# The MLP's residual in a two-block transformer kernel: turned by VectorE in 32 by 32 blocks and moved by transfers, in place of 32 transposes by TensorE

## The chip, the cores and the metric

The kernel runs on one core of a Trainium2 chip. The metric is the device time of one execution in microseconds; the median of three runs of the kernel before is 989.25 us (988.41 to 989.67). The profiled execution took 988.87 us, its span (first to last recorded instruction) 987.0 us, at a mean granted TensorE clock of 0.997 of full speed.

## The reference

The reference is two blocks on a sequence of 512 rows of 1024 features, float32. The first is a windowed attention with a gated spatial branch. The second puts a mixer ahead of an MLP. The change touches the last step of the second block alone:

```
h = h + y @ w_out[l]                        # x1 in this text
u = _rmsnorm(h, mlp_norm_g[l])
h = h + jnp.square(jax.nn.relu(u @ w_up[l])) @ w_down[l]
h = _rmsnorm(h, final_norm_g)
```

`w_up` is 1024 x 4096, `w_down` 4096 x 1024. The residual is the first `h` of the third line: x1, 512 rows by 1024 features. (The second block has 16 further rows at its front for the mixer; the MLP works on 512.)

## The kernel before

**Float32 products in parts.** Each operand is split into a high part (fp32r) and a low part, the difference to it, and a product is three matmuls: high by high, high by low, low by high. ScalarE casts the high part of each weight tile (`cast`), VectorE or GpSimd subtracts for the low part (`w_low`, `low`).

**The layout.** Up to the MLP, activations lie with features on partitions: x1 is `F3`, 128 features by 512 rows in each of eight slices `F3[:, n]`. The down product turns the layout: its result has rows on partitions, and so has the output. The residual must therefore be transposed before it can be added to the down product. It is put into `Y` (the memory `F1f`), which holds 128 rows by 4 x 1024 values: half of the rows r, half of the features c, tile of rows t, 512 features n.

**The MLP's order.** The hidden features are worked in four parts of 1024. In each part there are eight up tiles (`up_tile(part, n)`, 24 matmuls each), then seven down products (`down_tile(part, n, h)`, named P11, P_7, P12, P_5, P_6, P_3, P_4; 24 matmuls each), seven in place of eight since the 2 x 2 grid of halves is multiplied in Strassen's way. Sums and differences of operands for it are made by VectorE (`x_sums`, `w_sum`) and by accumulating loads that GpSimd issues (`w_sum` in `gpsimd_program`). VectorE drains each up tile from PSUM (`act`), ScalarE squares it (`act_square`), casts the operand's high part (`a_high`), VectorE makes the low part (`a_low`). Down products P11, P_7, P_5 and P_6 are gathered in `acc`, which lies in the memory `F4f`; P12 adds to `Y`. Their output copies are `out(part, n)` on VectorE.

**The residual before.** TensorE transposes x1 after the up tiles 3, 4, 5 and 6 of part 0, two slices of four 128 x 128 transposes each time (`residual` in `tensor_program`, line 941), into PSUM banks 6 and 7; ScalarE copies each into `Y` (`residual` in `scalar_program`, line 1481; in the profile its copies stand under the helper's line 1021 as Fm<-ps).

**What sets the order.** The order on each engine is written out by hand, and each engine does its list in order; semaphores by name tie them (`w.wait_ge(name, key)`). The first two down weights' high parts (tile `m` 0 and 1) go into `w_more`, which is the memory of `F3`; so their cast waits until x1 has been read for the last time (before: `residual_turned` 7). The first output copy, `out(0, P11)`, writes `acc[0]`. The down product P12 may begin when the output copies of P11 have emptied its banks (`down_free`). ScalarE's list for the stage is in the loop `for n in range(3, 8)`: a cast for up tile n + 2, the two residual copies, squares, and in rounds 5 and 6 `a_high` for P11 and P_7; then the casts of the down weights with squares 5 and 6 between.

**Other transfers in the stage.** SP loads weight blocks of 1 MB when the low parts that read the slot's old content are made (line 433), and quarters of w_down (lines 512, 520). GpSimd issues an accumulating load of 512 KB each between its low parts (line 2564). Earlier in the kernel, at line 508, SP loads the input x once more in pieces of 32 floats, four transfers of 32 x 128 such pieces, and VectorE turns them 32 by 32 (line 1976, `x_again`).

Of the kernel before, what the change touches and what calls it, by code (L numbers as in the profile page):

```python
# [117 lines left out]
J_IN2, J_CG, J_OUT2, J_UP = 82, 92, 96, 104  # L118
# [13 lines left out]
def build(nc, t):  # L132
    with ExitStack() as ctx:
# [150 lines left out]
        Z = X[:].rearrange("p k n -> p (k n)").rearrange("p (t c) -> p t c", t=4)  # L284

        Y = F1f.rearrange("p (r c t n) -> p r c t n", r=2, c=2, t=2)
        Hl_flat = Hl[:].rearrange("p k n -> p (k n)")
        by4 = lambda ap: ap.rearrange("p (k n) -> p k n", k=4)
        by2 = lambda ap: ap.rearrange("p (k n) -> p k n", k=2)
# [276 lines left out]
        def tensor_program(e, w):  # L566
# [363 lines left out]
                    mm = e.matmul(ps[:, 6, :], ones_r, x, start=(n == 0), stop=(n == 1))  # L930
                mm.then_inc(*b.done("mlp_row_sums", 0))

            def residual(n):
                bk = 7 - n % 2
                if n > 1:
                    w.wait_ge("residual_set", n - 2)
                elif n == 1:
                    w.wait_ge("mlp_mean", 0)
                w.wait_ge("x1_late", n)
                for i in range(4):  # L940
                    mm = e.transpose(ps[:, bk, 128 * i:128 * i + 128], F3[:, n, 128 * i:128 * i + 128], ident[:])  # L941
                mm.then_inc(*b.done("residual_turned", n))

            def down(part, n):

                xh, xl = x_slot(part, n)
# [25 lines left out]
            def down_free(part, n, r):  # L972

                if n == P_4:
                    return "residual_set", 7 - r
                if n == P_3:
                    return "drained", up_tile(0, r)
                if n in (P11, P_7):
                    return "drained", up_tile(part, (4 if n == P11 else 6) + r)
                last = {P12: P11, P_5: P_7, P_6: P12}[n]  # L980
                return ("kept", (last, r)) if part == 3 else ("down_out", (part, last, r))

            for part in range(4):
                for n in range(8):
                    if part == 0:
                        free = (("conv_low", n) if n < 2 else ("x1_late", n) if n < 4 else ("x1_late", n - 4) if n < 6
                                else ("drained", up_tile(0, n - 4)))
                    else:
                        free = (("down_out", (part - 1, P_5 if n < 2 else P_6, n % 2)) if n < 4 else
                                ("drained", up_tile(part, n - 4)))  # L990
                    product(up_tile(part, n), [[(up_bank(part, n), 0, 512)]], A8h, A8l, lambda k: ("u3_low", k), MLP_ORDER,
                            free=[free], tail=0 if part or n else 2)
                    if part == 0 and n == 2:
                        mlp_sums()
                    if part == 0 and 3 <= n < 7:
                        residual(2 * n - 6)
                        residual(2 * n - 5)
                for n in range(7 if part < 3 else 6):
                    down(part, n)

# [18 lines left out]
        def scalar_program(e, w):  # L1019
            def copy(out, src, scale=1.0):  # L1020
                return e.activation(out, src, ACT.Copy, scale=scale)  # L1021

            def cast(j):
                blk, i = tiles[j]
                if blk is not None:
                    w.wait_ge(f"raw_in{blk % 2}", blk)
                else:
                    part, n, h = i
                    if n in (P11, P12, P_3):
                        w.wait_ge(f"quarter{int(n != P11)}{int(n == P_3)}_in", part)  # L1030
                    else:
                        by_dve = n == P_4 or (n, h) == (P_6, 1)
                        w.wait_ge(*(("w_sum_v", (part, n, h)) if by_dve else (w_sum_name(n, h), (part, n))))
                m = turn_of(j)
                before = j - 3 if m < 2 else j - 5 if m == j - J_UP - 8 else j - 7
                if in_w_last(j):
                    w.wait_ge("lo", J_UP + 22 * 3 + 7)
                elif m in (0, 1):
                    w.wait_ge("residual_turned", 7)
                elif before >= 0:  # L1040
                    group = 1 if tiles[before][0] is None else {8: 0, 4: 1, 2: 3}[tile_rows(before)]
                    w.wait_ge("products", (before, group))
                copy(w_hi(j), raw_tile(j)).then_inc(*b.done("hi", j))
# [434 lines left out]
                    w.wait_ge("mlp_sum", n - 2)  # L1478
                e.activation(sq[n % 2] if n else sq[2], F3[:, m], ACT.Square).then_inc(*b.done("mlp_square", n))

            def residual(n):
                w.wait_ge("x1_late", 3)
                w.wait_ge("residual_turned", n)
                src = ps[:, 7 - n % 2, :].rearrange("p (r t c) -> p r t c", r=2, t=2)
                copy(Y[:, :, n // 4, :, 128 * (n % 4):128 * (n % 4) + 128], src).then_inc(*b.done("residual_set", n))

            def a_high(part, n):

                if n in (P11, P12, P_4):
# [27 lines left out]
            def keep(n):  # L1517

                for r in range(2):
# [4 lines left out]
                        copy(less[n][:, r], bank, -1.0).then_inc(*b.done("less", (n, r)))  # L1524
                    copy(kept[n][:, r], bank).then_inc(*b.done("kept", (n, r)))

            for n in range(3, 8):
                if n < 6:
                    cast(up_tile(0, n) + 2)
                if n < 7:  # L1530
                    residual(2 * n - 6)
                    residual(2 * n - 5)
                for i in {3: (0,), 4: (1, 2), 5: (3,), 6: (4,)}.get(n, ()):
                    act_square(0, i)
                if n in (5, 6):
                    a_high(0, n - 5)
            cast(down_tile(0, P11, 0))
            act_square(0, 5)
            cast(down_tile(0, P11, 1))
# [75 lines left out]
        def vector_program(e, w):  # L1615
# [689 lines left out]
            def act(part, n):  # L2305
                j = up_tile(part, n)
                if n == 0:
# [3 lines left out]
                e.scalar_tensor_tensor(X[:, n], ps[:, up_bank(part, n), :], 0.0, RB, ALU.max, ALU.mult).then_inc(  # L2311
                    *b.done("drained", j))

            def x_sums(part, n):

                one, other, old = {P_7: (x_half(1, 0), x_half(0, 0), None), P_5: (x_half(1, 0), x_half(1, 1), None),
                                   P_6: (x_half(0, 0), x_sum, P_5), P_3: (x_half(0, 1), x_sum, P_6)}[n]
                w.wait_ge("act_set", (part, 3 if n == P_7 else 7))
                if old is not None:
                    w.wait_ge("a_low", (part, old))  # L2320
                elif part:
                    w.wait_ge("a_low", (part - 1, P_3))
                e.tensor_tensor(x_operand(n), one, other, ALU.subtract).then_inc(*b.done("x_sum", (part, n)))
# [22 lines left out]
            def out(part, n):  # L2346

                for r in range(2):
# [2 lines left out]
                    w.wait_ge("products", (down_tile(part, n, 1), r))  # L2351
                    signal = b.done("down_out", (part, n, r))
                    if n != P12 and part == 0:
                        e.tensor_copy(y, bank).then_inc(*signal)
                    else:
                        w.wait_ge(*(("down_out", (part - 1, n, r)) if part else ("residual_set", 7)))
                        e.tensor_tensor(y, bank, y, ALU.add).then_inc(*signal)

            def last_sum():
# [14 lines left out]
            for part in range(4):  # L2374
                for n in range(8):
                    act(part, n)
                    if part == 3 and n < 6:
# [3 lines left out]
                        if n == 5:  # L2381
                            b.value["vector_step", "spread"] = b.count["vector_step"]
                    if n == 3:
                        x_sums(part, P_7)
                    if n == 4:
                        a_low(part, P11)
# [335 lines left out]
```

## Time and profile before

| | before |
|---|---|
| median of the runs | 989.25 us |
| profiled execution, its own time | 988.87 us |
| its span | 987.0 us |
| VectorE busy | 627.5 us |
| ScalarE busy | 470.6 us |
| GpSimd busy | 524.9 us |
| residual transposes of TensorE | 32, from 669.8 to 689.7 us |
| DMA, whole span | 117.49 MB, mean 119 GB/s |

Times in rows are microseconds from the span's start unless marked ns. PE is TensorE, DVE VectorE, ACT ScalarE, POOL GpSimd; SPq and ACTq are the issuing side of SyncE and ScalarE. A duration of a single matmul is longer than the distance to the next, since they overlap. DMA issues aren't counted as busy time of their engine. A DMA share of 1 means that the packets' times add up to all 16 DMA engines; since packets overlap it can pass 1.

### The profile page before, as it was taken

What the parts mean: (1) busy time and instruction counts of PE and PEld (TensorE: products, weight loads), DVE (VectorE), ACT (ScalarE), POOL (GpSimd) and SP (SyncE); (2) the same over time, 40 slices, a digit from 0 to 9 for tenths busy, and PEclk for the clock granted to TensorE, in tenths of its full rate; (3) what the DMA queues carried; (4) which work ended last, traced back from release to release, by engine and by line L of the source; (5) the groups of instructions that cost most, each with busy time, mean ns of one, the idle gap of its engine ahead of it and who ended that gap; (6) DMA issues with size and microseconds to landing.
All of it is one profiled execution on the core that took longest, in us unless ns stands there. A gap on an engine that the chain in (4) does not pass through costs nothing.

```text
span 987.0 us, 12665 instructions
## 1 busy us (share of the span) xinstructions
PE 976.6 (99%) x4827; PEld 827.5 (84%) x4827; DVE 627.5 (64%) x938; ACT 470.6 (48%) x746; POOL 524.9 (53%) x625
## 2 busy tenths in 40 slices
PE   9999999999999999999999999999999999999996
PEld 7888888888888888888899988888888888888885
DVE  5782257665373763274669999874962771595696
ACT  4554445554673223442334866554643443353464
POOL 4555555556555895555656778555056037018212
PEclk9999999999999999999999999999999999999998
DMA  7323221212353225623223123468558347536346
GB/s 238 102 78 126 85 87 44 85 41 68 107 175 124 86 86 134 146 87 127 65 86 107 46 74 118 125 237 193 149 175 197 107 147 185 149 87 182 53 85 171
DMA packets 109116, 117.49 MB, mean 119 GB/s; under 512 B 20434, under 2 KB 86512, under 8 KB 109056
## 3 DMA queue, kind: packets, MB, share of 16 engines
q1 hardware_dynamic: 102304, 102.20, 33.1%
q0 software_dynamic: 6448, 14.16, 8.4%
q8 instruction: 38, 0.62, 0.2%
q10 hardware_dynamic: 304, 0.33, 0.1%
q14 instruction: 22, 0.18, 0.1%
HBM read 110.91 MB, written 2.10 MB: 114 GB/s over the span
## 4 chain that ended last, share of the span: by engine, by line
PE 99%; DVE 0%; ACT 0%; DVEq 0%; issue 0%; ACTq 0%
PE ps L585 70%; PE ps L967 15%; PE ps L604 4%; PE ps L730 1%; PE ps L654 1%; PE ps L751 1%; PE ps L715 1%; PE ps L714 1%; PE ps L845 1%; PE ps L1013 1%; PE ps L792 1%; PE ps L637 0%; PE ps L630 0%; PE ps L941 0%; PE ps L879 0%; DVE X L2472 0%
## 5 line engine op out<-in xcount | busy, mean ns | idle before, releaser
L2523 POOL TENSOR_TENSOR wlo<-raw,whi 128x256 fp32r<-128x256 f32 x496 | 400.4, 860 | 216.6 <-ACT whi L1021 216.5
L585 PE MATMUL ps<-Hh,whi 128*128 128x512 f32 x512 | 201.6, 394 | 0.0
L585 PE MATMUL ps<-Hl,whi 128*128 128x512 f32 x512 | 199.5, 390 | 0.0
L1021 ACT ACTIVATE whi<-raw 128x1024 fp32r<-128x1024 f32 (+1 forms) x126 | 132.2, 1050 | 87.4 <-PE ps L585 51.4
L585 PE MATMUL ps<-Ah,whi 128*128 128x512 f32 (+1 forms) x496 | 164.3, 357 | 0.0
L585 PE MATMUL ps<-Al,whi 128*128 128x512 f32 (+1 forms) x496 | 163.5, 356 | 0.0
L585 PE MATMUL ps<-Hh,wlo 128*128 128x512 f32 x512 | 129.4, 389 | 0.0
L585 PEld LDWEIGHTS ps<-Hh,wlo 128*128 128x128 f32 x512 | 96.1, 188 | 20.0
L585 PEld LDWEIGHTS ps<-Hh,whi 128*128 128x128 f32 x512 | 96.2, 188 | 19.6 <-DVE Hl L1620 0.2
L585 PEld LDWEIGHTS ps<-Hl,whi 128*128 128x128 f32 x512 | 96.2, 188 | 19.2
L585 PE MATMUL ps<-Ah,wlo 128*128 128x512 f32 (+1 forms) x496 | 104.8, 356 | 0.0
L585 PEld LDWEIGHTS ps<-Ah,whi 128*128 128x128 f32 x496 | 88.0, 188 | 13.1
L585 PEld LDWEIGHTS ps<-Al,whi 128*128 128x128 f32 x496 | 87.9, 188 | 13.0
L585 PEld LDWEIGHTS ps<-Ah,wlo 128*128 128x128 f32 x496 | 83.3, 188 | 13.3
L2564 POOL DMA_DIRECT2D w_w<-in_w_down x16 | 19.5, 1216 | 118.3 <-DVE wlo L1620 50.9
L2311 DVE SCALAR_TENSOR_TENSOR X<-ps,Rb 128x512 f32<-128x512 f32 x32 | 21.8, 688 | 86.2 <-PE ps L585 85.3
L1623 DVE TENSOR_TENSOR tmp<-ps,Rb 128x512 f32<-128x512 f32 x25 | 17.2, 690 | 59.4 <-PE ps L585 59.4
L2534 POOL TENSOR_TENSOR P<-P,sm 128x1024 f32<-128x1024 f32 (+1 forms) x16 | 26.9, 1682 | 51.9 <-DVE sm L1813 51.9
L967 PE MATMUL ps<-whi,Hl 128*128 128x512 f32 x216 | 53.3, 389 | 0.0
L585 PE MATMUL ps<-Ah,w_more 128*128 128x512 f32 x160 | 50.2, 389 | 0.0
L967 PEld LDWEIGHTS ps<-whi,Hl 128*128 128x128 f32 x216 | 40.5, 188 | 8.4
L2523 POOL TENSOR_TENSOR w_more<-raw,w_more 128x256 fp32r<-128x256 f32 x40 | 30.9, 933 | 19.5 <-ACT w_more L1021 19.5
(371 smaller groups left out, 1662.8 us busy)
## 6 DMA issues: line engine op xcount, KB each, us to landing
raw<-in_w_in SPq DMA_DIRECT2D x29, 1024.0 KB, 5.3
raw<-in_w_up SPq DMA_DIRECT2D x16, 1024.0 KB, 5.6
Fm<-in_w_down SPq DMA_DIRECT2D x8, 1024.0 KB, 5.0
w_w<-in_w_down POOLq DMA_DIRECT2D x16, 512.0 KB, 5.7
raw<-in_w_in SPq DMA_DIRECT2D x14, 512.0 KB, 3.8
raw<-in_w_att_out SPq DMA_DIRECT2D x4, 1024.0 KB, 5.2
raw<-in_w_sg_out SPq DMA_DIRECT2D x4, 1024.0 KB, 5.2
raw<-in_w_o SPq DMA_DIRECT2D x4, 1024.0 KB, 5.1
```

The source lines that it names most:

```text
L585: mm = e.matmul(ps[:, bk, 0:c1 - c0], of(j)[:, k % kk, 128 * g:128 * g + 128], x[:, k, c0:c1], start=(start and n == 0), stop=(stop and n ...
L604: mm = e.matmul(ps[:, banks[r], :], x[:, k, 128 * r:128 * r + 128], of(j)[:, k % 2], start=(i == 0 and n == 0), stop=(i == 3 and n == 5))
L654: mm = e.matmul(ps[:, i, :], of(i)[:, k], x[:, k], start=(k == 0 and of is w_hi and x is Hh), stop=last)
L714: e.matmul(out, lhs, kdh[:, g, k0:k0 + W], start=True, stop=False)
L715: mm = e.matmul(out, lhs, kdl[:, g, k0:k0 + W], start=False, stop=True)
L967: mm = e.matmul(ps[:, down_bank(part, n, r), :], x[:, k, 128 * r:128 * r + 128], of(j)[:, k % 2], start=(first and fresh), stop=(last and ...
L1021: return e.activation(out, src, ACT.Copy, scale=scale)
L1623: e.tensor_tensor(out, ps[:, bk, :], R, ALU.mult).then_inc(*b.done("drained", j))
L2311: e.scalar_tensor_tensor(X[:, n], ps[:, up_bank(part, n), :], 0.0, RB, ALU.max, ALU.mult).then_inc(*b.done("drained", j))
L2523: ins = e.tensor_tensor(w_lo(j)[:, *cut], raw_tile(j)[:, *cut], f(w_hi(j))[:, *cut], ALU.subtract)
L2534: e.tensor_tensor(Pf[:, u, :, :, 0:W], Pf[:, u, :, :, 0:W], rb, ALU.mult).then_inc(*b.done("probs", i))
L2564: e.dma_start(w_sum3[h] if n == P_7 else quarter(0, 1, h), src, accum_op=ALU.add).then_inc(*b.done(w_sum_name(n, h), (part, n), 16))
```

## The change

TensorE's transposes and ScalarE's copies go. VectorE, after it has drained up tile 3 of part 0, turns x1 in 32 by 32 blocks from `F3` into `F4f` with sixteen instructions of 128 x 256. The blocks then stand on the right column but on the wrong partitions: block i of rows must go to partitions 32 i to 32 i + 31. Sixteen transfers within SBUF, issued by ScalarE, do that, each from 32 partitions to 32 partitions: 4 KB that lie together on the source's partition, written as 32 pieces of 128 bytes, 512 bytes apart. Eight stand ahead of `a_high(0, P11)` (round 5), eight behind `a_high(0, P_7)` (round 6), ahead of the casts of the down weights. These casts now wait for VectorE's last block (`residual_blocks` 7), and every first output copy of part 0 waits for the last transfer, as `acc` lies where the turned blocks were. Product P_4 of part 0 no longer waits for the residual's banks.

```diff
+        Y_pieces = F1f.rearrange("p (x c f) -> p x c f", c=4, f=32)
+        turned = F4f.rearrange("p (i x f) -> p i x f", i=4, f=32)
@@ tensor_program
-            def residual(n):
-                ...
-                for i in range(4):
-                    mm = e.transpose(ps[:, bk, 128 * i:128 * i + 128], F3[:, n, 128 * i:128 * i + 128], ident[:])
-                mm.then_inc(*b.done("residual_turned", n))
@@ down_free
                 if n == P_4:
-                    return "residual_set", 7 - r
+                    return "mlp_mean", 0
@@ the parts' loop of tensor_program
-                    if part == 0 and 3 <= n < 7:
-                        residual(2 * n - 6)
-                        residual(2 * n - 5)
@@ cast
                 elif m in (0, 1):
-                    w.wait_ge("residual_turned", 7)
+                    w.wait_ge("residual_blocks", 7)
@@ scalar_program
-            def residual(n):
-                ...
+            def move_residual(cs):
+                w.wait_ge("residual_blocks", 7)
+                for c in cs:
+                    for i in range(4):
+                        e.dma_start(Y_pieces[32 * i:32 * i + 32, :, c], turned[32 * c:32 * c + 32, i]).then_inc(
+                            *b.done("residual_in", (c, i), 16))
             for n in range(3, 8):
                 if n < 6:
                     cast(up_tile(0, n) + 2)
-                if n < 7:
-                    residual(2 * n - 6)
-                    residual(2 * n - 5)
                 for i in {3: (0,), 4: (1, 2), 5: (3,), 6: (4,)}.get(n, ()):
                     act_square(0, i)
+                if n == 5:
+                    move_residual((0, 1))
                 if n in (5, 6):
                     a_high(0, n - 5)
+                if n == 6:
+                    move_residual((2, 3))
@@ vector_program
+            def residual(n):
+
+                to = F4f.rearrange("p (i r c t m f) -> p r c t i m f", i=4, r=2, c=2, t=2, m=4)
+                of = F3[:, n].rearrange("p (r t i f) -> p r t i f", r=2, t=2, i=4)
+                w.wait_ge("products", (J_UP - 1, 3))
+                for r in range(2):
+                    signal = b.done("residual_blocks", n) if r else step()
+                    e.transpose(to[:, r, n // 4, :, :, n % 4], of[:, r]).then_inc(*signal)
@@ out
                     if n != P12 and part == 0:
+                        w.wait_ge("residual_in", (3, 3))
                         e.tensor_copy(y, bank).then_inc(*signal)
                     else:
-                        w.wait_ge(*(("down_out", (part - 1, n, r)) if part else ("residual_set", 7)))
+                        w.wait_ge(*(("down_out", (part - 1, n, r)) if part else ("residual_in", (3, 3))))
                         e.tensor_tensor(y, bank, y, ALU.add).then_inc(*signal)
@@ the parts' loop of vector_program
                     if n == 3:
+                        if part == 0:
+                            for m in range(8):
+                                residual(m)
                         x_sums(part, P_7)
```

## Rows read from the trace of the kernel before

**Rows 1.** The page's first section: busy time, share of the span, instructions of each engine

```profile
PE 976.6 (99%) x4827; PEld 827.5 (84%) x4827; DVE 627.5 (64%) x938; ACT 470.6 (48%) x746; POOL 524.9 (53%) x625
```

**Rows 2.** Chain of waits in order of time: start, length, engine, line, instructions

```profile
670.00 0.87 PE ps L941 x8
...
695.39 38.08 PE ps L967 x168
733.47 43.52 PE ps L585 x192
```

**Rows 3.** Timeline of ScalarE: start, length, operation; in brackets idle time before and releaser

```profile
676.84 1.09 ACT L1021 ACTIVATE Fm<-ps 128x512 f32<-128x512 f32 x2 [3.81 <-PE ps L941]
...
678.85 1.06 ACT L1021 ACTIVATE whi<-raw 128x1024 fp32r<-128x1024 f32 x1
...
691.98 1.06 ACT L1021 ACTIVATE w_more<-Fm 128x1024 fp32r<-128x1024 f32 x1
```

**Rows 4.** Timeline of VectorE

```profile
669.45 2.48 DVE L2311 SCALAR_TENSOR_TENSOR X<-ps,Rb 128x512 f32<-128x512 f32 x4 [0.78 <-ACT Rb L1512]
684.81 3.85 DVE L2323 TENSOR_TENSOR x_sum<-X 128x1024 f32<-128x1024 f32 x1 [12.89 <-ACT X L1515]
...
698.41 0.68 DVE L2311 SCALAR_TENSOR_TENSOR X<-ps,Rb 128x512 f32<-128x512 f32 x1
...
704.34 1.28 DVE L2354 COPY Fm<-ps 128x512 f32<-128x512 f32 x2
...
726.09 1.76 DVE L1620 TENSOR_TENSOR Hl<-X,Hl 128x1024 fp32r<-128x1024 f32 x1
```

**Rows 5.** Line 1976, VectorE's transposes of x: duration in ns, minimum, median, maximum

```profile
L1976 DVE STREAM_TRANSPOSE Fm<-Fm x8: 696/704/705, 431.8 to 465.3; 128x512 f32<-128x512 f32 x8
```

**Rows 6.** Timeline of SP and line 508: issues of x's blocks, time to landing

```profile
387.24 0.65 SPq L508 DMA_DIRECT2D Fm<-in_x  x1
387.93 5.29 SPq L508 DMA_DIRECT2D Fm<-in_x  x1
...
398.09 2.51 SPq L508 DMA_DIRECT2D Fm<-in_x  x1
...
DMA to landing us min/median/max: 6.5/8.5/11.0
```

**Rows 7.** DMA packets in 387.2 to 393.22, 400.6 to 405, 399 to 401

```profile
DMA packets 3946, 1.42 MB, mean 236 GB/s; under 512 B 2922, under 2 KB 3946, under 8 KB 3946
...
DMA packets 5320, 0.86 MB, mean 195 GB/s; under 512 B 5119, under 2 KB 5320, under 8 KB 5320
...
DMA packets 3348, 0.44 MB, mean 218 GB/s; under 512 B 3347, under 2 KB 3347, under 8 KB 3347
```

**Rows 8.** Stretches: length, busy time of each engine, granted clock, DMA share, GB/s

```profile
678.80:682.30 3.50, 3.50 (x17) 2.88 (x16) 0.00 (x0) 1.11 (x2) 2.26 (x4) 1.00 1.09 239
682.30:685.20 2.90, 2.90 (x18) 2.50 (x17) 0.39 (x1) 1.99 (x4) 1.69 (x3) 1.00 0.02 3
685.20:688.60 3.40, 3.40 (x16) 2.80 (x16) 3.40 (x2) 0.67 (x1) 2.37 (x4) 1.00 1.01 152
688.60:692.50 3.90, 3.90 (x23) 3.30 (x22) 2.77 (x5) 2.96 (x5) 1.22 (x1) 1.00 0.93 286
692.50:695.50 3.00, 3.00 (x15) 2.48 (x14) 3.00 (x4) 3.00 (x5) 0.00 (x0) 1.00 0.85 155
```

**Rows 9.** Timeline of SP: issue of a load of 1,024 pieces

```profile
687.60 0.37 SPq L433 DMA_DIRECT2D raw<-in_w_up  x1
```

**Rows 10.** Timeline of TensorE: the start of product P12

```profile
706.11 1.98 PE L967 MATMUL ps<-whi,x_part 128*128 128x512 f32 x8
```

**Rows 11.** DMA packets in 678.8 to 682.3, 685.2 to 688.6, 688.6 to 692.5

```profile
DMA packets 589, 0.84 MB, mean 239 GB/s; under 512 B 25, under 2 KB 337, under 8 KB 589
...
DMA packets 255, 0.52 MB, mean 152 GB/s; under 512 B 3, under 2 KB 3, under 8 KB 255
...
DMA packets 1081, 1.12 MB, mean 286 GB/s; under 512 B 27, under 2 KB 1044, under 8 KB 1081
```

More of the change, by code:

```diff
@@ L931, in mlp_sums @@
                 mm.then_inc(*b.done("mlp_row_sums", 0))
-            def residual(n):
[L934 to L939, printed above, removed]
-                for i in range(4):
-                    mm = e.transpose(ps[:, bk, 128 * i:128 * i + 128], F3[:, n, 128 * i:128 * i + 128], ident[:])
-                mm.then_inc(*b.done("residual_turned", n))
             def down(part, n):
@@ L1479, in mlp_square @@
                 e.activation(sq[n % 2] if n else sq[2], F3[:, m], ACT.Square).then_inc(*b.done("mlp_square", n))
-            def residual(n):
[L1482 to L1485, printed above, removed]
             def a_high(part, n):
```

## The prediction

> **What bounds the kernel now.** I read the page first: TensorE is busy 976.6 of 987.0 us [rows 1], so an instruction taken from TensorE is worth its full time if nothing else then comes late. Next the chain of waits in order of time, for the first part of the MLP [rows 2]: it lies on TensorE without a break, up tiles, four groups of eight residual transposes, down products. Then the timelines of ScalarE and VectorE there [rows 3, 4], to see what stands ready how long before TensorE asks; the earlier load of x in blocks, as the nearest thing to the new transfers [rows 5 to 7]; and the stretches of the DMA engines in which these would run [rows 8, 11].
>
> **What is removed.** From the first transpose at 670.00 to the first down product at 695.39 are 25.39 us [rows 2]; in them stand four up tiles. Eight later ones without transposes take 43.52 us, 5.44 each, so four are 21.76. The 32 transposes with what they disturb cost 3.63 us. TensorE would be ready for the down products at 691.8. Eight PSUM copies leave ScalarE (two take 1.09 us [rows 3], four pairs 4.4 us), and with them its waits for transposes.
>
> **VectorE's new work.** After the fourth drain, which ends at 669.45 + 2.48 = 671.93, VectorE idles 12.89 us before the difference of 684.81 [rows 4]. Sixteen 32 by 32 transposes of 128x256 go there. The same instruction on 128x512 takes 0.70 us [rows 5]; by half of it, 0.35, they need 5.6 us and end at 677.5. As the output here is in 32-element runs, the upper bound is the whole 0.70: 11.2 us, ending at 683.1; the lower is a little under 0.35. I take 0.35, since elements set the time of the near rows. The idle time hides it; without that cover each us would move ScalarE's transfers. The difference P_7 follows them at 677.5 instead of 684.81, since square 3 no longer stands behind copies. Of it and the three drains behind it none is late: even at 3.85 us [rows 4] it ends at 681.4.
>
> **ScalarE's new work is where I see the price.** Without copies, cast 7 (at 678.85 before [rows 3]) waits only for its up tile, at 675.3; with square 3 it ends at 676.9, and the first eight transfers wait for the turned blocks until 677.5. Each transfer moves 32 x 32 pieces of 128 B, so sixteen are 16,384 pieces, 2 MB. The trace has exactly that amount: x is loaded in four transfers of 4,096 pieces each. The first issue took 0.65 us, the second 5.29 and the last, at 398.09, 2.51, from 387.24 to 400.60 in all, landing in 6.5 to 11.0 us [rows 6]: the queue took something over 4,096 pieces, and then the issuing engine stood. When the second issue ended (393.22), 2,922 pieces had been moved of 8,192: 5,270 in the queue. When the fourth ended, 5,119 were left. Undisturbed, 3,347 pieces move in 2 us, 1,670 per us at a DMA share of about 1.36 [rows 7], 1,215 per us and unit of share.
>
> So I give ScalarE's queue room for 5,200. The first eight (8,192 pieces) are issued when 3,000 are moved, the second eight when 11,200 are. What the engines are already doing [rows 8]: shares 1.09, 0.02, 1.01, 0.93 and 0.85 in stretches from 678.8 (first data, 1.3 us after the issue, my estimate) to 695.5. If the pieces get what is left up to 1.35: 1,100; 4,690; 1,400; 1,990; 1,820. Sum at 685.2: 5,800, so the first eight are issued by 683.5; then a_high 0 (1.06), square 4 (0.6) and a_high 1 (1.06) run to 686.2, and the second eight begin. The sum is 11,010 at 695.5; ScalarE is free at **695.6**. Only then can it cast the first down weight, which now starts at 691.98 [rows 3] and ends at 693.04.
>
> **What waits for ScalarE.** Behind the transfers stand that cast, square 5, the other down casts, and square 6; for them wait VectorE's w_low, its last drain, the difference P_5, and the output copies. Before, from the cast's end (693.04) VectorE needed 5.4 us to the last drain at 698.41, and 11.9 to the end of the first output copy (704.34 + 0.64) [rows 4]; P12 began on TensorE at 706.11 [rows 10], 1.1 us after that copy. With ScalarE free at T, TensorE begins P12 at T + 1.06 + 11.9 + 0.1 = T + 13.1. That equals 706.1 at T = 693.1: the break-even. The whole 3.63 comes if T is at most 689.4. Later a_low of P_4 ends at 726.09 + 1.76 = 727.85 [rows 4], just where P_4 begins (706.11 + 4 x 5.44 = 727.87), its second operand 0.45 us on; up to 0.6 us more can be lost there. The sum: 695.6 - 693.1 = 2.5 us more than before, 0 to 0.6 for the later place; I take 2.4. Against the profiled execution's own 988.87 us that is 991.3; the median of the runs, 989.25, is 0.38 above it, so **991.6**.
>
> Bounds for T: if an issue never waits, eight cost 8 x 0.41 us (0.37 of a 1,024-piece load and a gap [rows 9]) to 8 x 0.69 (0.65 of the first issue in rows 6): 677.5 + 3.3 to 5.5, the two a_high and a square 2.7, again 3.3 to 5.5: 686.8 to 691.2. At the other end the others' packets go first, and pieces have the idle time and little more (rival F): T = 698.1. With transposes at 0.70, T would pass 700. With transposes at 0.70, T would pass 700.
>
> **Landing.** By the forecast's rates all pieces are moved near 699; out(P11) needs them at T + 1.06 + 11.3 = 708. VectorE's new wait is free there.
>
> **Rivals.**
> A, the whole gain: the queue of ScalarE takes eight transfers of 1,024 at a time, or pieces within SBUF move much faster than those from HBM in rows 7. For it: room for 5,200 is nearly two thirds of eight, and the engines idle at 682.3 to 685.2 [rows 8]. Against: the issues of rows 6. T at most 689.4; 988.87 - 3.63 + 0.38 = 985.6. The Trainium skill (DMA: Bandwidth & Descriptors, Why small descriptors are slow) says that copies within SBUF are spared the small-packet penalty; by it T would lie nearer the break-even or below. No run here shows it.
> B, others give way: in contested stretches the pieces get half the engines, 820 per us. 2,870 by 682.3, some 8,190 at 686.4 (all issued), 10,000 at 688.6, 11,200 at 690.1. T - 693.1 = -3.0: 986.3.
> C, ScalarE isn't held, but the pieces land late, one for each packet of others: 6,920 at 695.5 and the other 9,460 in 5.7 us, 701.2, some 703 with the next part's loads. VectorE's output copy is due at 704.34 - 3.63 = 700.7, and stands 2 to 3 us; P12 with it: 3.6 - 2.5, a gain of 1: 988.2.
> D, the forecast: ScalarE held, T 694.5 to 697, TensorE standing before the first down product for 4 to 6 us. That is the slower side; it decides from T = 693.1 on. Whether so long a stand also lowers TensorE's granted clock no row of this stage shows (it is 1.00 in all of rows 8); if it did, a few slow matmuls more would come on top.
> F, one piece for each packet of the others: the contested stretches of rows 8 hold 589, 255, 1,081 [rows 11] and, for the last, some 250 packets, the idle one room for 4,750 pieces, together 6,920 at 695.5; 4,280 more take 2.6 us: T = 698.1, 5.0 to 5.6 us more, 994.3 to 994.9. For it: beside other packets the share only rises to 1.09, not to the 1.36 of pieces alone. Against: pieces are so short that several may slip in. The Trainium skill (same page, Queues, rings and completion order) has each DMA engine take turns between its queues packet by packet, which is this rival; no row has 128-byte pieces beside another queue, so the trace neither bears it out nor refutes it.
> E, around the break-even, T 691.5 to 694.5.
>
> **Chances.** D 0.28, F 0.15, A 0.19, B 0.13, C 0.12, E 0.13. About 0.2% (2 us) is what can be told from no change. Faster by more: A and B, 0.32. Within: C and E, 0.25. Slower: D and F, 0.43. The range 985.4 to 995.2 takes in A and F's end; D alone runs from 990.6 to 993.8.
>
> **What would show it.** Right: transposes on VectorE of about 0.35 us from 671.9; among ScalarE's issues several near 0.4 us and then ones of over 1 us; the cast of the first down weight near 695.6; TensorE idle behind that cast for some 4 us, and again about 1 us before P12; parts 1 to 3 as before. Wrong: sixteen issues of 0.4 us, no idle time of TensorE (A), or a VectorE wait at its first output copy for the DMA (C). Transposes of 0.7 us would push everything 5 us later, and break the forecast on its other side.

## The result and the profile after

The changed kernel takes 999.11 us (median of three executions; 997.82 to 1000.62) against 988.99 before: ratio 1.0103, 95% interval 1.0089 to 1.0117, slower by 10.1 us. A second job with the same kernel gave 1000.16 us against 989.2, slower by 11.0 (ratio 1.0111 [1.0092, 1.0129]), so the change costs some 10.5 us. The forecast was slower by 2.4 with 995.2 as the upper end, so the direction was right and the size far off. The execution profiled in the first job ran at a granted clock of 0.75 throughout (1226.99 us) and is left out, and all rows of after are from the second job (a_again; profiled execution 999.38 us, span 997.6).

The page's first section of after, columns as in [rows 1]:

```profile
PE 974.4 (98%) x4795; PEld 824.3 (83%) x4795; DVE 629.3 (63%) x954; ACT 466.4 (47%) x738; POOL 525.4 (53%) x625
```

TensorE has 32 instructions fewer and is busy 2.2 us less, in a span 10.6 us longer: it stands 23.2 us in all, where it stood 10.4 before. The timeline of TensorE has the place (start, length, in brackets the idle time before):

```profile
704.12 7.16 PE L960 MATMUL ps<-w_more,Hl 128*128 128x512 f32 x24 [12.54 <-issue]
...
716.55 1.98 PE L960 MATMUL ps<-whi,x_part 128*128 128x512 f32 x8
```

The first down product starts at 704.12 after 12.54 us of idle time. The second row is the start of P12, 706.11 before [rows 10]: 10.44 of the 10.6 us are there by then. The timeline of ScalarE has the cause:

```profile
677.04 14.13 ACTq L1515 DMA_DIRECT2D Fm<-Fm  x8
691.21 1.06 ACT L1011 ACTIVATE Hl<-X 128x1024 fp32r<-128x1024 f32 x1 [14.33 <-issue]
691.29 2.04 ACTq L1515 DMA_DIRECT2D Fm<-Fm  x1
692.18 0.61 ACT L1499 ACTIVATE X<-X 128x512 f32<-128x512 f32 x1
692.70 1.04 ACT L1011 ACTIVATE Hl<-x_sum 128x1024 fp32r<-128x1024 f32 x1
693.36 9.56 ACTq L1515 DMA_DIRECT2D Fm<-Fm  x7
702.96 1.06 ACT L1011 ACTIVATE w_more<-Fm 128x1024 fp32r<-128x1024 f32 x1 [9.22 <-issue]
```

Line 1515 is the new transfer. From 677.04 to 702.96 ScalarE does 2.7 us of work and issues for the rest. The last row is the cast of the first down weight, at 691.98 before [rows 3]: 10.98 us later. The chain of waits shows the first eight issues one by one, each the time for which it held ScalarE:

```profile
677.04 0.73 ACTq L1515
...
677.81 0.69 ACTq L1515
...
678.52 3.69 ACTq L1515
...
682.24 1.27 ACTq L1515
...
683.54 0.69 ACTq L1515
...
684.26 0.71 ACTq L1515
...
685.00 1.88 ACTq L1515
...
686.91 4.26 ACTq L1515
```

Four are near 0.7 us, the others hold ScalarE for 1.27 to 4.26 us. What moves meanwhile is in the views of the DMA packets; one group of rows each for 682.5 to 683.5, 686 to 688 and 692 to 694. The very first row counts all packets; the others give packets, MB and share of time by queue (q10 is ScalarE's, q0 GpSimd's, q1 SyncE's):

```profile
DMA packets 1645, 0.21 MB, mean 209 GB/s; under 512 B 1644, under 2 KB 1644, under 8 KB 1645
q10 hardware_dynamic: 1643, 0.21, 131.7%
...
q0 software_dynamic: 114, 0.23, 69.0%
q10 hardware_dynamic: 238, 0.03, 11.2%
...
q1 hardware_dynamic: 561, 0.57, 89.6%
q10 hardware_dynamic: 503, 0.06, 21.0%
```

Alone, and with the queue full, 1,643 pieces move in 1 us, nearly the 1,670 of [rows 7]. Beside GpSimd's accumulating load it is 238 in 2 us, two for each of its packets; beside SyncE's load of a weight 503 in 2 us, 0.9 for each packet. Summed from the packet records (of ScalarE's queue, without the 4-byte records that end a transfer), 1,790 pieces had moved at 683, 4,430 at 685.2, 6,660 at 691, 7,830 at 695 and 14,500 at 703. When ScalarE came free at 702.96 some 1,900 were left.

Last, the stretches 690 to 695, 695 to 700, 700 to 705 and 705 to 710 of after, columns as in [rows 8]:

```profile
690.00:695.00 5.00, 1.58 (x7) 0.96 (x6) 2.70 (x3) 2.52 (x3) 1.22 (x1) 0.86 1.15 271
695.00:700.00 5.00, 0.00 (x0) 0.00 (x0) 0.86 (x2) 0.00 (x0) 0.00 (x0) 0.50 0.93 158
700.00:705.00 5.00, 0.88 (x2) 0.82 (x3) 0.95 (x1) 2.04 (x3) 0.00 (x0) 0.50 0.91 155
705.00:710.00 5.00, 5.00 (x19) 3.94 (x19) 4.46 (x5) 2.92 (x5) 0.00 (x0) 0.78 0.34 108
```

While TensorE stands, its granted clock falls to 0.50, which is 1.2 GHz, and it is back at 1.00 only after it has worked for some us. P11 takes 6.99 us (704.12 to 711.11) instead of 5.44.

### The profile page after: what moved, and what is told of

The parts are those of the page before. It is cut to its first block, busy times and chain, and to the rows that moved or that the text cites. A ratio compares the mean times of both kernels' runs of the same rounds, so it can differ in the third digit from the quotient of the medians.

```text
span 1225.2 us, 12625 instructions
## 1 busy us (share of the span) xinstructions
PE 1209.0 (99%) x4795; PEld 893.7 (73%) x4795; DVE 622.2 (51%) x954; ACT 468.6 (38%) x738; POOL 518.2 (42%) x625
## 4 chain that ended last, share of the span: by engine, by line
PE 99%; issue 1%; DVE 0%; DVEq 0%; ACT 0%; ACTq 0%
PE ps L589 70%; PE ps L960 15%; PE ps L608 4%; PE ps L734 1%; PE ps L658 1%; PE ps L755 1%; PE ps L719 1%; PE ps L718 1%; PE ps L849 1%; PE ps L1003 1%; PE ps L796 0%; PE ps L634 0%; PE ps L641 0%; PE ps L617 0%; PE ps L883 0%
## 5 line engine op out<-in xcount | busy, mean ns | idle before, releaser
L2528 POOL TENSOR_TENSOR wlo<-raw,whi 128x256 fp32r<-128x256 f32 x496 | 392.8, 832 | 363.0 <-ACT whi L1011 363.0
L589 PE MATMUL ps<-Hh,whi 128*128 128x512 f32 x512 | 236.6, 462 | 0.0
L589 PE MATMUL ps<-Hl,whi 128*128 128x512 f32 x512 | 234.0, 457 | 0.0
L589 PE MATMUL ps<-Ah,whi 128*128 128x512 f32 (+1 forms) x496 | 191.0, 413 | 0.0
L589 PE MATMUL ps<-Al,whi 128*128 128x512 f32 (+1 forms) x496 | 190.4, 412 | 0.0
L589 PE MATMUL ps<-Hh,wlo 128*128 128x512 f32 x512 | 159.4, 455 | 0.0
L589 PE MATMUL ps<-Ah,wlo 128*128 128x512 f32 (+1 forms) x496 | 128.2, 410 | 0.0
L589 PEld LDWEIGHTS ps<-Al,whi 128*128 128x128 f32 x496 | 95.6, 203 | 27.8
L960 PE MATMUL ps<-whi,Hl 128*128 128x512 f32 x216 | 65.9, 456 | 0.0
L589 PE MATMUL ps<-Ah,w_more 128*128 128x512 f32 x160 | 60.3, 456 | 0.0
```

Of the source, the lines that this page charges most:

```text
L589: mm = e.matmul(ps[:, bk, 0:c1 - c0], of(j)[:, k % kk, 128 * g:128 * g + 128], x[:, k, c0:c1], start=(start and n == 0), stop=(stop and n ...
L960: mm = e.matmul(ps[:, down_bank(part, n, r), :], x[:, k, 128 * r:128 * r + 128], of(j)[:, k % 2], start=(first and fresh), stop=(last and ...
L2528: ins = e.tensor_tensor(w_lo(j)[:, *cut], raw_tile(j)[:, *cut], f(w_hi(j))[:, *cut], ALU.subtract)
```

## The experiments

Where nothing else is said, the diff is against the changed kernel, and the times of before on the same chips are 989.2 to 989.3.

**The change again** (a_again), for a profile at the full clock:

> The changed kernel once more, for a trace at the full clock. Held (my theory): ScalarE's two groups of eight issues hold it some 10 us each (11.2 and 11.7 us in the first trace, which was taken at a granted clock of 0.75); TensorE then stands 7 to 10 us before the first down product, and its clock falls for some us behind the stand; time 998 to 1001 us. Rival (the transfers land late, and VectorE's first output copy waits for them): TensorE's stand would be before P12, and no long stand before the first down product.

The rows above. 1000.16 us.

**No transfers** (e_no_moves: the residual stays where VectorE turned it). What is the removal worth alone?

```diff
-                if n == 5:
-                    move_residual((0, 1))
...
-                if n == 6:
-                    move_residual((2, 3))
...
-                        w.wait_ge("residual_in", (3, 3))
+                        w.wait_ge("residual_blocks", 7)
...
```

> The sixteen transfers are left out (the residual is not added rightly), VectorE's transposes and all the rest stay. Both theories: what the removal of the 32 transposes is worth by itself, 3.6 us: 985.2 to 985.9 where the kernel before has 989.2. If VectorE's transposes cost anything on the path (a third view), it is 987 or more.

985.98 us, ratio 0.9965 [0.9952, 0.9979], 0.1 above the upper end I gave. P12 starts at 703.30, 2.8 us before its time in [rows 10]. So the transposes with what hangs on them were worth 3.2 us (2.7 by the spans), near the 3.63 of the forecast, and the transfers cost 14 us (1000.16 against 985.98).

**SyncE issues them** (e_sp_moves: all sixteen, between its loads for part 1). If ScalarE's being held is the cause, another holder frees it.

```diff
+                if part == 1:
+                    w.wait_ge("residual_blocks", 7)
+                    for c in range(4):
+                        for i in range(4):
+                            e.dma_start(Y_pieces[32 * i:32 * i + 32, :, c], turned[32 * c:32 * c + 32, i]).then_inc(
+                                *b.done("residual_in", (c, i), 16))
...
-                if n == 5:
-                    move_residual((0, 1))
...
-                if n == 6:
-                    move_residual((2, 3))
```

> All sixteen transfers issued by SyncE, between the two weight loads of part 1; ScalarE issues none. Held: ScalarE is free, SyncE stands in its place 15 to 20 us, the next 1 MB load starts at about 697 instead of 687.6 and is not needed before 738; all pieces land near 698 to 700, just before the first output copy at 700.7: 985.5 to 987.5. Late landing as the cause: still 995 or more, with VectorE waiting at its first output copy.

991.87 us, ratio 1.0027 [1.0017, 1.0036]; the ten runs spread from 988.58 to 993.3, and the profiled one is the lowest. That lies between the two forecasts: 8.3 us of the loss are gone with the same pieces in flight, so these were ScalarE's time, but not all of it is gone. Of the 2.6 to 5.9 us still missing the profile shows this; timelines of SyncE, VectorE, GpSimd, ScalarE and TensorE:

```profile
677.12 20.87 SPq L534 DMA_DIRECT2D Fm<-Fm  x16
698.04 0.68 SPq L437 DMA_DIRECT2D raw<-in_w_up  x1
...
700.11 1.29 DVE L2358 COPY Fm<-ps 128x512 f32<-128x512 f32 x2 [2.38 <-DMA Fm<-Fm]
...
702.95 1.20 POOL L2571 DMA_DIRECT2D w_w<-in_w_down  x1 [12.26 <-DVE w_more L1614]
...
712.76 2.00 ACT L1017 ACTIVATE whi<-w_w 128x1024 fp32r<-128x1024 f32 x2 [6.74 <-DMA w_w<-in_w_down]
...
715.82 2.09 PE L966 MATMUL ps<-whi,Hl 128*128 128x512 f32 x8 [2.39 <-DVE Fm L2361]
```

SyncE is held 20.9 us, so its loads for part 1 come out together from 698.04. VectorE waits 2.38 us for the pieces at its first output copy, yet TensorE does not stand there (P12 starts at 702.39). It stands at 715.82: GpSimd's accumulating load, issued at 702.95 among those bunched loads, lands 9.8 us later, the cast behind it waits, and VectorE with its later output sum.

**The same sixteen transfers in 4 KB runs** (e_large_pieces: same bytes, engine and count, 512 pieces instead of 16,384). Is it the number of pieces or the number of transfers?

```diff
-                        e.dma_start(Y_pieces[32 * i:32 * i + 32, :, c], turned[32 * c:32 * c + 32, i]).then_inc(
+                        whole = F1f.rearrange("p (c n) -> p c n", c=4)
+                        e.dma_start(whole[32 * i:32 * i + 32, c], turned[32 * c:32 * c + 32, i].rearrange("p x f -> p (x f)")).then_inc(
```

> The same sixteen transfers by ScalarE at the same places with the same bytes, but written 4 KB together per partition (512 instead of 16,384 pieces in all; the residual comes to the wrong places). Held by pieces in the queue: sixteen issues of about 0.4 us, no stand, 985.5 to 986.5. Rival (each issue costs ScalarE 0.9 to 1.9 us whatever it moves): the stand stays, 996 or more.

988.95 us, ratio 0.9999 [0.999, 1.0008]. Timeline of ScalarE, and the DMA packets from 686 to 688.5, all of them these 4 KB runs and the records that end a transfer:

```profile
677.49 7.35 ACTq L1516 DMA_DIRECT2D Fm<-Fm  x8
...
692.29 1.06 ACT L1011 ACTIVATE w_more<-Fm 128x1024 fp32r<-128x1024 f32 x1 [4.87 <-issue]
...
DMA packets 205, 0.56 MB, mean 223 GB/s; under 512 B 69, under 2 KB 69, under 8 KB 205
q10 hardware_dynamic: 205, 0.56, 96.2%
```

The pieces cost 11.2 us of the 14. The other 3 were missed by both theories: twelve of the issues took 0.54 to 0.67 us, not 0.4, and the other four 2.23, 1.20, 1.64 and 1.79 us; the first of these is the third in a row, with only 64 pieces ahead of it. ScalarE is free at 692.29, and P12 starts at 705.36; T + 13.1 gives 705.4.

**The first eight alone** (e_first_eight: the second group is left out, half of the residual with it).

```diff
-                if n == 6:
-                    move_residual((2, 3))
...
-                        w.wait_ge("residual_in", (3, 3))
+                        w.wait_ge("residual_in", (1, 3))
...
```

> Only the first eight of the sixteen transfers, ScalarE's second group is left out (half of the residual is missing). Theory (time follows T, the time at which ScalarE is free for the first down cast, from the break-even at 693.1 of the prediction on): the first group still holds ScalarE until 691.2 as in the full-clock trace of the changed kernel, a_high, square 4 and a_high bring T to 693.9; with the stand of TensorE some 1 to 2 us over the kernel before: 990 to 991.5. Rival (the cost is the traffic of the pieces, not ScalarE's hold): half of the changed kernel's 11 us, 994 to 995.

990.49 us (986.86 to 991.62), ratio 1.0014 [1.0005, 1.0023], as the theory had it. The profiled execution is one of the faster ones (989.38). In it the issues took 12.65 us, the first down cast ran at 692.71, TensorE stood 1.73 us, and P12 started at 706.15; T + 13.1 gives 705.8. The second group is the larger part of the loss, 9.7 us by the medians: there the hold has no cover left.

**Eight transfers of 2,048 pieces** (e_double). Does the queue's room count pieces or transfers?

```diff
-                    for i in range(4):
-                        e.dma_start(Y_pieces[32 * i:32 * i + 32, :, c], turned[32 * c:32 * c + 32, i]).then_inc(
...
+                    for i in (0, 2):
+                        at, o = divmod(2 * c + i // 2, 2)
+                        to = F1f.rearrange("p (x f) -> p x f", f=64)[32 * at:32 * at + 32, :, 32 * o:32 * o + 32]
+                        e.dma_start(to, turned[32 * c:32 * c + 32, i:i + 2].rearrange("p i x f -> p (i x) f")).then_inc(
+                            *b.done("residual_in", (c, i + 1), 16))
```

> The same 16,384 pieces of 128 bytes by ScalarE at the same two places, but in eight transfers of 2,048 pieces instead of sixteen of 1,024 (the residual comes to the wrong places). If the queue has room for two transfers, whatever they hold: the third issue is the first one held, with some 4,000 pieces in the queue; the first group ends near 685 instead of 691.2 and ScalarE is free near 698: 993 to 996. If it has room for some 2,000 pieces: the second issue is held already, the first group ends near 691, time as the changed kernel's, 998 to 1001.

999.88 us, ratio 1.0111 [1.0097, 1.0125]. Timeline of ScalarE, the second issue by itself among its rows; then the packets of its queue from 677 to 703.35, and those of the change from 677 to 702.96, the 4-byte records counted in:

```profile
677.15 8.71 ACTq L1517 DMA_DIRECT2D Fm<-Fm  x4
...
677.93 3.79 ACTq L1517 DMA_DIRECT2D Fm<-Fm  x1
...
685.98 5.04 ACTq L1517 DMA_DIRECT2D Fm<-Fm  x1
...
691.05 12.26 ACTq L1517 DMA_DIRECT2D Fm<-Fm  x3
703.35 1.06 ACT L1011 ACTIVATE w_more<-Fm 128x1024 fp32r<-128x1024 f32 x1 [14.92 <-issue]
```

```profile
q10 hardware_dynamic: 13626, 1.73, 44.6%
...
q10 hardware_dynamic: 14692, 1.85, 45.7%
```

Neither forecast fits whole: the time and the hold of the second issue are those of the second, the end of the first group is that of the first. The first four issues end at 685.86, 5.3 us before the same pieces were out in the change; by the packet records 4,820 of the 8,192 had moved, so 3,400 were in the queue, where the change had 1,440 at the end of its first eight. At the end of the fifth issue 2,900 were left, and when ScalarE came free at 703.35 2,850 (16,384 less 13,530), against 1,900 in the change. So the room is no fixed number of pieces, it grows with the size of a transfer. At the ends of the held issues 65 to 96 pieces were left in e_large_pieces, with 32 in a transfer, 1,350 to 2,500 in the change, with 1,024, and 2,190 to 3,460 here, with 2,048; in the load of x, with 4,096, it was 5,270 and 5,119 [rows 6, 7]. In transfers that is 3, 2.5, 1.7 and 1.3 at the most, so it is no fixed number of transfers either; what it counts stays open. T came out the same although more pieces were left, since fewer had moved by then; why they moved more slowly here no run tells.

**GpSimd's loads beside them cut to 4 KB** (e_quiet: the sums of part 0's down weights lack their second terms).

```diff
+                to = w_sum3[h] if n == P_7 else quarter(0, 1, h)
+                if part == 0:
+                    to, src = to[0:16, 0:1, 0:64], src[0:16, 0:1, 0:64]
...
```

> The changed kernel, but the five accumulating loads that GpSimd issues for part 0 move 4 KB each instead of 512 KB (so part 0's summed weights are wrong). If ScalarE is held because the pieces pass one for one beside those loads' packets: the first group ends near 684 (eight issues at the floor of 0.7), ScalarE is free near 692 to 694: 988 to 991. If the hold is a property of the transfers alone: ScalarE is free after 700 as before, 998 or more.

991.93 us, ratio 1.0027 [1.0016, 1.0037]: 8.2 us of the loss come back when five transfers that have nothing to do with the change are taken away. Timelines of ScalarE and TensorE, and the stretch 695 to 700:

```profile
677.21 11.24 ACTq L1515 DMA_DIRECT2D Fm<-Fm  x8
...
690.73 3.70 ACTq L1515 DMA_DIRECT2D Fm<-Fm  x5
694.48 1.06 ACT L1011 ACTIVATE w_more<-Fm 128x1024 fp32r<-128x1024 f32 x1 [3.45 <-issue]
...
695.63 8.57 PE L960 MATMUL ps<-w_more,Hl 128*128 128x512 f32 x24 [3.87 <-issue]
```

```profile
695.00:700.00 5.00, 4.37 (x10) 3.47 (x11) 3.95 (x4) 4.42 (x6) 0.00 (x0) 0.50 0.30 44
```

It is 0.9 us above the upper end I gave, and the rows say why. T = 694.48 alone makes +1.4 (P12 at 707.6); but after a stand of 3.87 us the clock is at 0.50 in the whole stretch, and the 24 matmuls take 8.57 us where e_no_moves has 5.60. VectorE's output copy ran at 706.71, and TensorE came to P12 only at 709.48. The first eight issues ended at 688.5 and not near 684; one of them alone, at 683.14, held 4.53 us while a load of SyncE moved.

**The second eight behind the four down casts** (e_second_late). Does a later place help?

```diff
-                if n == 6:
-                    move_residual((2, 3))
...
+            move_residual((2, 3))
```

> The change with ScalarE's second eight transfers put behind its four down casts instead of among them. The first eight are issued where the change has them (14.1 us), so the down product P11 starts 13 to 14 us after 677, near 692 to 694 instead of 704. Theory (the time goes by how long ScalarE is held ahead of each thing TensorE waits for): the hold of the second eight now stands ahead of ScalarE's later work and of the output copies that need the pieces; P11 and P12 come 7 to 9 us earlier than in the change, and the pieces land after 705, so that VectorE's output copies wait for them: 992 to 996. Rival 1 (the second eight then cost nothing): as e_first_eight, 990 to 991. Rival 2 (what is held once is lost whole, wherever it stands): as the change, 999 to 1001.

1000.38 us, ratio 1.0111 [1.0098, 1.0124]; the time is that of rival 2. Timelines of ScalarE and TensorE:

```profile
699.13 9.87 ACTq L1515 DMA_DIRECT2D Fm<-Fm  x5
709.04 0.63 ACT L1499 ACTIVATE X<-X 128x512 f32<-128x512 f32 x1 [11.20 <-issue]
...
694.06 2.06 PE L960 MATMUL ps<-w_more,Hl 128*128 128x512 f32 x8 [1.77 <-issue]
...
715.08 3.75 PE L960 MATMUL ps<-whi,x_part 128*128 128x512 f32 x8 [9.40 <-DVE Fm L2355]
```

P11 starts at 694.06 as expected, but square 7, the next work in ScalarE's list, stands behind the transfers until 709.04. VectorE's difference for P_5 (`tmp<-X`, 709.71) and, behind that, its first output copy (714.25) wait for it. P12 starts at 715.08, 1.5 us earlier than in the change, and gives that back: after 9.40 us of standing its first eight matmuls take 3.75 us instead of 1.98. So a hold isn't lost wherever it stands, as rival 2 says; it is lost here because the next work behind it is waited for as well.

**The blocks turned and moved in two halves, by SyncE** (e_two_halves: the first half of the transposes in VectorE's idle time before the mean).

```diff
+            def move_residual(h):
+                w.wait_ge("residual_blocks", (7, h))
+                for c in range(4):
+                    for i in (2 * h, 2 * h + 1):
+                        e.dma_start(Y_pieces[32 * i:32 * i + 32, :, c], turned[32 * c:32 * c + 32, i]).then_inc(
+                            *b.done("residual_in", (c, i), 16))
...
+            for m in range(8):
+                residual(m, 0)
...
-                                residual(m)
+                                residual(m, 1)
```

> All transfers by SyncE, in two halves: VectorE turns half of the blocks (rows' blocks 0 and 1 of each four) in its idle time before the mean at 664.5 and the other half where the change has them; eight transfers go after the load of final_g (about 667), eight between the two weight loads of part 1. ScalarE issues none. Theory: every hold falls on SyncE, the second half lands near 690, ten us before the first output copy: 985.5 to 986.8, faster than both kernels. Rival (the pieces take the DMA engines from loads that are on the path, whoever issues them): 988 or more.

988.37 us, ratio 0.9998 [0.9989, 1.0006], 1.6 above the upper end of the theory and in the range of the rival. Better than one group by 3.5 us, and still 2.4 short of the gain of e_no_moves. SyncE is held until 694.23 and its loads follow at 694.26, 698.31, 698.92 and 699.42; GpSimd's load of 702.16 lands after 9.9 us; TensorE stands 1.74 us at 715.17.

**SyncE's loads behind GpSimd's** (e_loads_later, the diff against e_two_halves).

```diff
+                    w.wait_ge("w_sum0", (0, P_6))
```

> This is the kernel of e_two_halves (the turned blocks in two halves, the first in VectorE's idle time ahead of the mean, all transfers issued by SyncE) with SyncE's loads for part 1 held back until GpSimd's accumulating load w_sum0 of (0, P_6) has landed, so that they no longer move beside it. In e_two_halves that load was issued at 702.16 and landed at 712.08, 9.9 us, where 5 to 6 us is usual for it, and the cast behind it waited. Theory (what is left of the gain is lost to loads that bunch behind the held queue and slow GpSimd's load): the load lands in 5 to 7 us, the run gives 985.5 to 987.0, faster than before by 0.2 to 0.4%, and the gain of e_no_moves (985.98) is there nearly whole. Rival 1 (the landing of the pieces at the first output copies, 1.6 us, is what costs, and the load's slide is covered later): no better than e_two_halves, 988 to 988.6. Rival 2 (the loads of part 1 are now late themselves, and TensorE waits for a weight at the start of part 1): 990 or more, with idle time of TensorE behind a DMA there.

985.44 us (985.03 to 985.88), ratio 0.9962 [0.995, 0.9974], as the theory had it and the fastest of all, before included. Timelines of VectorE, GpSimd, ScalarE, SyncE and TensorE:

```profile
701.73 1.29 DVE L2360 COPY Fm<-ps 128x512 f32<-128x512 f32 x2 [2.08 <-DMA Fm<-Fm]
...
704.57 1.20 POOL L2573 DMA_DIRECT2D w_w<-in_w_down  x1 [9.88 <-DVE w_more L1613]
...
710.22 2.01 ACT L1022 ACTIVATE whi<-w_w 128x1024 fp32r<-128x1024 f32 x2 [2.58 <-DMA w_w<-in_w_down]
...
710.21 0.38 SPq L437 DMA_DIRECT2D raw<-in_w_up  x1
...
702.73 1.99 PE L971 MATMUL ps<-whi,x_part 128*128 128x512 f32 x8
```

GpSimd's load lands in 5.6 us, though it starts 2.4 us later than in e_two_halves; the pieces still come 2.08 us late for VectorE, and no TensorE row from 690 to 800 shows idle time. The span, 984.1, is that of the kernel without transfers (984.3): their whole price is gone.

**The same hold on e_sp_moves** (e_sp_later, the same line added there).

> The kernel of e_sp_moves (all sixteen transfers of the change issued by SyncE, the transposes where the change has them) with the same hold of SyncE's part-1 loads behind GpSimd's accumulating load of (0, P_6). In e_sp_moves two waits were seen: VectorE's first output copy 2.4 us for the pieces, and 9.8 us for GpSimd's load. Theory (both count, one behind the other): the second goes and the first stays, 987.5 to 989.5, that is 2.5 to 4 us less than e_sp_moves' 991.87 and 1.5 to 2.5 us above e_loads_later. Rival 1 (only the loads count): 985.5 to 987, the same as e_loads_later. Rival 2 (only the pieces' landing counts): 991 to 992.5, unchanged.

986.42 us (984.92 to 989.74), ratio 0.9973 [0.9964, 0.9981], 1.1 below the lower end of the theory and in the range of rival 1 (only the loads count). VectorE's first output copy waits 4.35 us for the pieces, of which TensorE feels 1.00 before P12, at 703.64; the stand near 716 is gone. So the bunched loads were nearly the whole remainder, 5.5 us by the medians, and the late landing costs about 1.

## Why the prediction was right in direction and wrong in size

**Removal: right.** 3.2 us instead of 3.63 (e_no_moves).

**VectorE: right.** The sixteen transposes took 5.33 us, 0.33 each (5.6 forecast), and ended at 677.0 (677.5). The difference behind them took 1.57 us, well inside its slack.

**The mechanism: right, as D named it.** ScalarE is held by its own issues; TensorE stands before the first down product; parts 1 to 3 are as before (10.44 of 10.6 us arise before P12). Two runs show it: the same pieces issued by SyncE cost 8.3 us less, and without any transfer the loss is not there.

**T: the term that failed.** Forecast 695.6, measured 702.96, 7.4 us of a miss of some 8. The first eight were to be out by 683.5 and were by 691.2. Two sentences carry it. "I give ScalarE's queue room for 5,200": at 702.96 some 1,900 pieces were left. With 5,200, ScalarE would have been free when 11,200 had moved, which by the packet records was near 700.7; so the room is some 2.3 of the 7.4 us. The load of x has 4,096 pieces in a transfer, and the room doesn't carry over from it as a number of pieces (e_double). "The pieces get what is left up to 1.35": they got far less. The forecast had 11,010 moved by 695.5, and the trace has 7,920. Of the 3,090 that are missing, 1,370 are so already at 685.2 (5,800 forecast, 4,430 moved): the first piece moved at 679.39, 2.35 us after the first issue and not 1.3, which no row had shown, and in the nearly idle stretch 682.3 to 685.2 3,740 moved and not 4,690. The other 1,720 are missing in the contested stretches to 695.5, where 3,490 moved and not 5,210. e_quiet shows the sharing directly: without GpSimd's loads T falls to 694.5, by 8.5 us.

**Rival F was nearer in the sharing** and still came out too low. One to two pieces for each packet of the others is what the rows show. That its 6,920 at 695.5 is near the 7,920 is partly luck: in the contested stretches 4,180 pieces moved where it had some 2,175, in the idle one 3,740 where it had 4,750. It kept the room of 5,200, and it took 1,670 pieces per us from [rows 7] for the rest. Between 695 and 700 only 2,500 moved in 5 us, beside the tail of GpSimd's load of 691.67, and behind that some 1,400 per us, about the pace of the issues (1,024 pieces in 0.74 us). With room for 1,900 the rival's own sum gives 14,480 - 6,920 = 7,560 more, 4.5 us at 1,670: T = 700.0, and +6.9 instead of +5.0. The turn-taking of each DMA engine between its queues, which the Trainium skill states (DMA: Bandwidth & Descriptors, Queues, rings and completion order), agrees with these ratios. The same section has about 9 to 17 descriptors drained at each turn, which is not the rival's one piece; the ratios neither bear that out nor refute it, since they don't say how many pieces pass in a row.

**The bound below was no bound.** "If an issue never waits" gave T from 686.8 to 691.2. With 512 pieces in place of 16,384 ScalarE came free at 692.29: four of the sixteen issues hold even then. So rival A, at 0.19 and with T at most 689.4, was out of reach of sixteen such issues on ScalarE, and B's T of 690.1 too. The Trainium skill's sentence that copies within SBUF are spared the small-packet penalty (same page, Why small descriptors are slow) was to speak for A. The traces are in line with it: alone the 128-byte pieces moved at 209 GB/s, the 4 KB runs of e_large_pieces at 223. But the same pieces from HBM made 218 [rows 7], so it gave A nothing; A failed by the issues and by the sharing.

**The break-even formula: right.** T + 13.1 gives P12 at 716.06 for the change (716.55 measured), 705.8 for e_first_eight (706.15), 705.4 for e_large_pieces (705.36). It doesn't hold where the clock or another wait comes last: 707.6 for e_quiet (709.48).

**The clock: left out of the sum.** The prediction said that some slow matmuls could come on top. They did: P11 took 1.55 us more than at full clock in the change, of which 0.5 is left at P12, because VectorE's copy was late as well; in e_quiet 3.0 us, of which 1.9 is left at P12.

**Landing: right only in what followed.** VectorE's first output copy (715.19) waited for no piece, but the last pieces moved at 704.6 and not near 699; with ScalarE so late that cost nothing.

## What to carry to other kernels

A DMA of many small pieces costs the engine that issues it for as long as the pieces need to move, less what its queue still holds at the end (1,900 pieces in the change, 2,850 with transfers twice as large): price it by the rate that is left beside every other transfer of that stretch, and issue it from an engine with that much idle time ahead of its next consumer. Then look at what stands behind it in that engine's queue: loads that were spread out come out bunched, and slow a transfer elsewhere that somebody does wait for. Holding them back explicitly was worth 2.9 us in one version and 5.5 in the other. Together with the move to SyncE and the split in two halves it turned a change that lost 10.5 us into one that gains 3.8.

## What the runs showed of the hardware that I had not expected

- An issue of a transfer of 32 partitions within SBUF took 0.54 to 0.76 us where it was not held, on ScalarE and on SyncE alike, against 0.37 for the 1 MB load of a weight [rows 9]. The third in a row held 2.23 us with 64 pieces ahead of it (e_large_pieces), so a queue can hold its issuer with hardly any data in it.
- 128-byte pieces within SBUF moved at 1,640 per us alone (209 GB/s), no faster than those of [rows 7], and at 120 to 250 per us beside one other transfer.
- In e_quiet TensorE stood for 3.87 us; its granted clock was 1.00 up to 694 and 0.50 from 696 to 700, and the next 24 matmuls took 8.57 us instead of 5.60. After it had stood 1.73 us (e_first_eight) and 1.77 us (e_second_late) the granted clock was still 1.00, and 8 matmuls took 2.08 and 2.06 us.
- Between 698.5 and 700 of the change the pieces moved at only 520 per us, with the DMA engines at 0.47 of their time and ScalarE held until 699.21. In e_quiet it was 164 in the 1 us from 680.5, with four packets of other queues, so sharing isn't the cause. What held them there no run tells; it stays open.
